# Down projections of 16 experts as three fp32r products, with remainders formed on GpSimd and weight tiles cut by rows

## The chip, the core and the metric

The kernel runs on one core of one Trainium2 chip, as one program. The core has five engines with queues of their own: TensorE (PE), VectorE (DVE), ScalarE (ACT), GpSimd (POOL) and SyncE (SP). Each works through its queue in order; between queues only semaphores order the work. The metric is the device time of one execution in microseconds, as the median of the runs shown. Lower is better.

## The reference

The model is one block of diffusion-style layers (a Fourier branch, a bidirectional mLSTM and, last in the block, a mixture of experts) followed by two attention layers. All of it is float32. The change touches only the mixture of experts. `h` is 1024 rows of 1024 columns, there are 16 experts, and each takes the 128 rows that score it highest:

```python
def expert_choice(h, w_router, w_gate, w_up, w_down):
    b, l, _ = h.shape
    cap = CAP_FACTOR * l // N_EXPERTS                      # 128 rows
    aff = jax.nn.softmax(jnp.einsum('bld,de->ble', h, w_router).astype(jnp.float32), axis=-1)
    vals, idx = lax.top_k(jnp.swapaxes(aff, 1, 2), cap)
    bidx = jnp.arange(b)[:, None, None]
    xs = h[bidx, idx]
    hid = jax.nn.silu(jnp.einsum('becd,edf->becf', xs, w_gate)) * jnp.einsum('becd,edf->becf', xs, w_up)
    y = jnp.einsum('becf,efd->becd', hid, w_down) * vals[..., None].astype(h.dtype)
    return jnp.zeros_like(h).at[bidx, idx].add(y)

x = x + ga2 * expert_choice(hx2, w_router, w_gate_e, w_up_e, w_down_e)
```

Each of `w_gate`, `w_up` and `w_down` is 1024 x 1024 floats (4 MB) for each expert, 12 MB of weights for an expert.

## The kernel before, in words

The order of the work is written out by hand: each engine has its own program, in which an expert is a function `turn(e, more)`, called for expert 1, looped over experts 2 to 14 (`Fori`), and called for expert 15 (`more` is false there, as no expert follows). Expert 0 has gate and up alone ahead of the turns, and `down(16)` ends the stage.

**Tiles.** An expert's weights come in six tiles of 2 MB, numbered j: 0 and 1 gate, 2 and 3 up, 4 and 5 down. Tile j is the column half j % 2 of its matrix with all 1024 rows: 128 partitions x 8 row blocks (k) x 512 columns. `MRAW[j]` is its place; three lie in `ring`, two in `hidden`, one in `pair`. SP loads tile j of the next expert once PE has finished the product with tile j of this one (L758 to L797), in two DMAs of 1 MB. In turn e the down tiles are those of expert e-1.

**Three products.** A gate or up tile is multiplied in fp32r (a float32 rounded for a faster pass of PE) with remainders, whose sum stands for the float32 product. ACT rounds the weights, `high(e, j)`, into `MHIGH[j % 2]`, in four pieces of 128 x 1024 (L1711). DVE subtracts the rounded weights from the raw ones, `low(e, j)` (L2252), in the same four pieces, in place: `MLOW[j]` is the memory of `MRAW[j]`. The gathered rows x are split in the same way into XSH (L1702, ACT) and XSL (L2244, DVE). PE then forms, for each k, xh x high (L1250), xh x low (L1251) and xl x high (L1252), all accumulated in one PSUM bank (`split_product`). There are only two `MHIGH` buffers, so `high(e, j)` for j of 2 or more waits until the product with tile j-2 is done (`moe_high_free`).

**Down.** The down product is float32 (L293, in `group`): hidden rows transposed (`hidT`) times `MRAW[4]` into bank 4, then times `MRAW[5]` into bank 5, 8 matmuls each, and each is two records in the profile.

**PE's turn e:** four products with gate and up tiles of expert e; 8 transposes of the gathered rows of expert e+1 (L1261); down of expert e-1; 8 transposes of the hidden rows of expert e (L1268).

**DVE's turn e:** low of tiles 1, 2, 3; two multiplications of silu(gate) by up (L2259, `hidden_of`); half of the evacuation of the x transposes (L2238) and XSL (L2244); `output(e-1, 0)`, the scaled first half of the down result (L2269, waits for `moe_d`); low of tile 0 of expert e+1; `output(e-1, 1)`; half of the hidden transposes (L2263).

**ACT's turn e:** high of tile 1; silu of gate half 0 (L1719); high 2; silu of half 1; high 3; the other half of the x evacuation (L1693) and XSH (L1702); high 0 of expert e+1; the other half of the hidden transposes (L1715).

**POOL's turn e:** copy the next expert's row numbers (L885) and issue the gather of its rows (L887); wait for both outputs (`moe_y`); copy the row numbers of expert e-1 (L889) and issue the scatter that adds its results to the rows in memory (L891); wait until the scatter has landed (`moe_sct`), which so stands ahead of the next gather.

## Time and profile before

| | us |
|---|---|
| runs of the kernel before | 3163.53, 3164.49, 3170.97 |
| median | 3164.49 |
| the profiled execution, its time | 3172.3 |
| its span, from first to last instruction | 3170.5 |
| expert stage, first gate matmul (L1250) to the last output (L2269) | 1056.9 to 1667.5 |
| busy in the whole span: PE, DVE, ACT, POOL | 2892.3, 1612.7, 1301.3, 120.2 |
| one turn of the loop (L1261 at 1298.69 to L1261 at 1336.12) | 37.43 |

The page's busy shares are means over the whole program. For a change in one stage the views by stretch, by waits and in order of time say more: a row of the timeline gives the start of a group of equal instructions, the time from the first start to the last end, engine, line, what is written and what is read, the count, and in brackets for how long the engine sat idle before it and what ended that. Instructions that overlap are counted from start to start, so four subtractions with a span of 1.22 us each take 4.62 together.

### The profile page before, as it was taken

What the parts mean: (1) busy time and instruction counts of PE and PEld (TensorE: products, weight loads), DVE (VectorE), ACT (ScalarE), POOL (GpSimd) and SP (SyncE); (2) the same over time, 40 slices, a digit from 0 to 9 for tenths busy, and PEclk for the clock granted to TensorE, in tenths of its full rate; (3) what the DMA queues carried; (4) which work ended last, traced back from release to release, by engine and by line L of the source; (5) the groups of instructions that cost most, each with busy time, mean ns of one, the idle gap of its engine ahead of it and who ended that gap; (6) DMA issues with size and microseconds to landing.
All of it is one profiled execution on the core that took longest, in us unless ns stands there. A gap on an engine that the chain in (4) does not pass through costs nothing.

```text
span 3170.5 us, 37695 instructions
## 1 busy us (share of the span) xinstructions
PE 2892.3 (91%) x13850; PEld 2054.6 (65%) x13858; DVE 1612.7 (51%) x3148; ACT 1301.3 (41%) x2426; POOL 120.2 (4%) x168
## 2 busy tenths in 40 slices
PE   7999999999995699999994988898999988999998
PEld 3454467588875566666663765576667775776677
DVE  1217546234366666666644549463643557536433
ACT  2201235223233455445534537553642447436421
POOL 0000000000000010101000000000000000000000
PEclk9999999999996799999997999899999999999999
DMA  9420000122325599999975200200012200200121
GB/s 356 153 80 0 27 27 1 61 99 101 143 104 206 187 352 364 365 367 362 358 247 159 47 14 15 54 27 32 24 54 106 93 2 21 73 17 18 54 80 53
DMA packets 176889, 388.56 MB, mean 123 GB/s; under 512 B 7253, under 2 KB 8309, under 8 KB 176481
## 3 DMA queue, kind: packets, MB, share of 16 engines
q1 hardware_dynamic: 157920, 318.79, 28.7%
q0 software_dynamic: 18672, 67.72, 6.5%
q8 instruction: 97, 1.59, 0.2%
q14 instruction: 56, 0.45, 0.0%
q10 hardware_dynamic: 144, 0.01, 0.0%
HBM read 354.98 MB, written 31.51 MB: 122 GB/s over the span
## 4 chain that ended last, share of the span: by engine, by line
PE 84%; DVE 6%; ACT 4%; DMA 3%; issue 2%; SPq 1%; DVEq 0%; POOL 0%; POOLq 0%; ACTq 0%
PE psum L293 20%; PE psum L707 7%; PE psum L709 7%; PE psum L708 7%; PE psum L1250 4%; PE psum L1252 4%; PE psum L1251 4%; PE psum L1368 4%; PE psum L1386 3%; PE psum L1196 3%; PE psum L1195 3%; PE psum L1194 3%; PE psum L1415 2%; PE psum L1463 2%; PE psum L1465 2%
## 5 line engine op out<-in xcount | busy, mean ns | idle before, releaser
L708 PE MATMUL psum<-ring_r,kctx_r 128*128 128x512 f32 (+1 forms) x544 | 214.0, 393 | 0.0
L708 PE MATMUL psum<-ring_r,cols_r 128*128 128x512 f32 (+1 forms) x544 | 213.6, 393 | 0.0
L1812 ACT ACTIVATE ring<-ring,att 128x256 f32<-128x256 f32 (+7 forms) x256 | 173.7, 679 | 66.1 <-DVE att L2385 66.1
L1368 PE MATMUL psum<-wide 64*128 64x512 f32 (+2 forms) x704 | 155.2, 524 | 22.7 <-DVE att L2385 19.7
L293 PE MATMUL psum<-hidden,ring 128*128 128x512 f32 x384 | 167.5, 597 | 6.0 <-DVE wide L2126 4.0
L2252 DVE TENSOR_TENSOR ring_r<-ring,pair_r 128x1024 fp32r<-128x1024 f32 x128 | 148.1, 1219 | 23.7 <-ACT pair_r L1711 23.7
L1251 PE MATMUL psum<-ring_r,wide_r 128*128 128x512 f32 x384 | 151.3, 394 | 0.0
L1386 PE MATMUL psum<-ident,ring 128*128 128x128 f32 x640 | 120.1, 295 | 26.8 <-ACT sel_wT L1824 16.2
L1386 PEld LDWEIGHTS psum<-ident,ring 128*128 128x128 f32 x640 | 68.8, 143 | 105.4 <-issue 71.4
L293 PEld LDWEIGHTS psum<-hidden,ring 128*128 128x128 f32 x384 | 73.4, 192 | 97.0 <-issue 94.8
L1194 PE MATMUL psum<-small_r,ring_r 128*128 128x512 f32 x320 | 125.8, 393 | 0.8 <-DVE pair L2142 0.8
L1196 PE MATMUL psum<-small_r,ring_r 128*128 128x512 f32 x320 | 126.3, 395 | 0.0
L585 DVE TENSOR_TENSOR ring_r<-ring,ring_r 128x1024 fp32r<-128x1024 f32 x48 | 58.8, 1225 | 129.6 <-ACT ring_r L582 129.2
L1711 ACT ACTIVATE pair_r<-ring 128x1024 fp32r<-128x1024 f32 x128 | 124.5, 1048 | 0.0
L708 PEld LDWEIGHTS psum<-ring_r,kctx_r 128*128 128x128 f32 x544 | 104.9, 193 | 22.4
L708 PEld LDWEIGHTS psum<-ring_r,cols_r 128*128 128x128 f32 x544 | 103.9, 191 | 21.7
L707 PE MATMUL psum<-small_r,kctx_r 128*128 128x512 f32 (+1 forms) x240 | 101.0, 421 | 16.0 <-issue 7.7
L293 PE MATMUL psum<-pair,wide 128*128 128x512 f32 x256 | 112.6, 592 | 1.2 <-DMA pair<-in_w_down 1.2
L293 PE MATMUL psum<-hidden,wide 128*128 128x512 f32 x256 | 112.6, 593 | 1.0 <-DVE wide L2263 1.0
L707 PE MATMUL psum<-small_r,cols_r 128*128 128x512 f32 (+1 forms) x240 | 98.8, 412 | 15.2 <-DVE wide_r L676 13.8
L1250 PE MATMUL psum<-pair_r,wide_r 128*128 128x512 f32 x256 | 102.8, 402 | 7.0 <-DVE wide_r L2244 3.9
L1465 PE MATMUL psum<-wide_r,ring_r 128*128 128x512 f32 x256 | 101.9, 398 | 0.0
(452 smaller groups left out, 6759.8 us busy)
## 6 DMA issues: line engine op xcount, KB each, us to landing
ring<-in_w_gate SPq DMA_DIRECT2D x64, 1024.0 KB, 9.3
ring<-in_w_up SPq DMA_DIRECT2D x32, 1024.0 KB, 9.7
hidden<-in_w_up SPq DMA_DIRECT2D x32, 1024.0 KB, 9.4
hidden<-in_w_down SPq DMA_DIRECT2D x32, 1024.0 KB, 7.3
pair<-in_w_down SPq DMA_DIRECT2D x32, 1024.0 KB, 7.7
ring<-in_w_ada SPq DMA_DIRECT2D x24, 1024.0 KB, 12.1
ring<-in_w_in SPq DMA_DIRECT2D x24, 1024.0 KB, 7.3
ring<-in_even_w_in SPq DMA_DIRECT2D x16, 1024.0 KB, 16.0
```

Source lines behind the costliest of these rows:

```text
L293: mm = pe.matmul(outp, l, r, start=(i == 0), stop=(i == len(pairs) - 1))
L707: self.eng.matmul(outp, XHIGH[b][:, k, :], whigh(key, k)[:, 0:wd], start=(k == 0), stop=False)
L708: self.eng.matmul(outp, XHIGH[b][:, k, :], low[:, k, 0:wd], start=False, stop=False)
L709: mm = self.eng.matmul(outp, XLOW[b][:, k, :], whigh(key, k)[:, 0:wd], start=False, stop=(k == KT - 1))
L1194: pe.matmul(outp, w, high[:, j, :], start=(j == 0), stop=False)
L1196: mm = pe.matmul(outp, lows[:, k, span(c)], high[:, j, :], start=False, stop=(j == kn - 1))
L1250: pe.matmul(outp, xh[:, k, :], high, start=(k == 0), stop=False)
L1251: pe.matmul(outp, xh[:, k, :], low[:, k, :], start=False, stop=False)
L1368: mm = pe.matmul(bank(2 * (q % 2) + h)[:, 0:n], qT2[row, c, span(b)], kT2[row, 0 if name == "C" else c, k:k + n], start=True, stop=not dia ...
L1386: mm = pe.transpose(bank(4)[:, span(k)], sv[:, span(k)], ident[:])
L1465: mm = pe.matmul(bank(j % 4), low[:, k, span(c)], GHIGH[:, k, :], start=False, stop=(k == KT - 1))
L1812: act.activation(sv, sv, ACT.Exp, bias=nmx[:, q:q + 1], scale=-1.0, accum_out=esum[:, r:r + 1]).then_inc(S(name + "_e"), 1)
```

## The change

The changed kernel cuts every matrix by rows: tile j is the row half j % 2, 4 row blocks in full length of 1024 columns, so that a piece of 128 x 1024 is one row block, and both tiles of a matrix add to both of its banks. `split_product` takes, for each piece, both column halves. All that follows gate (silu) or up or down therefore waits for the second tile (`moe_g`, `moe_u`, `moe_d` at 2).

The down product becomes three fp32r products as well: `MSPLIT` is 6, ACT rounds tiles 4 and 5 too, and POOL forms their remainders (L903 of the changed kernel), signalled by `mw_lowd`. The transposed hidden rows are split into HDH (ACT, L1736) and HDL (DVE, L2289). In the last down product, that of turn 16, which no gate and up stand beside, ACT's jobs are numbered 0 and 1.

POOL's wait for the scatter's landing moves from the end of its turn to a place just ahead of the next scatter, so that the next gather is issued without it. The first turn is written out ahead of the loop on ACT and POOL.

```diff
+        def rows_of_tile(v):
+            return v.rearrange("p (k n) -> p k n", n=D)
...
-        MSPLIT = 4
+        MSPLIT = 6
...
+        def moe_lows(eng, e, j, p):
+
+            if j < 4 and not (isinstance(e, int) and e == NEXP):
+                eng.wait_ge(S("mw_low"), e * 16 + (4 * j + p + 1))
+            else:
+                eng.wait_ge(S("mw_lowd"), e * 8 + (4 * (j % 4) + p - 7))
...
-                ms = slice((j % 2) * HALF, (j % 2 + 1) * HALF)
-                w = w[e, :, ms].rearrange("(k p) n -> p k n", p=P) if isinstance(e, int) else \
-                    w[bass.ds(e, 1), :, ms].rearrange("e (k p) n -> p (e k) n", p=P)
-                for k0 in (0, 4):
-                    sp.dma_start(MRAW[j][:, k0:k0 + 4, :], w[:, k0:k0 + 4, :]).then_inc(S(f"ring_full{MRING[j] if j < RING else j}"), 16)
+                rs = slice((j % 2) * HALF, (j % 2 + 1) * HALF)
+                w = w[e, rs, :].rearrange("(k p) n -> p k n", p=P) if isinstance(e, int) else \
+                    w[bass.ds(e, 1), rs, :].rearrange("e (k p) n -> p (e k) n", p=P)
+                for k0 in (0, 2):
+                    sp.dma_start(MRAW[j][:, k0:k0 + 2, :], w[:, k0:k0 + 2, :]).then_inc(S(f"ring_full{MRING[j] if j < RING else j}"), 16)
...
+                for q in range(2):
+                    j = q if isinstance(e, int) and e == NEXP else 4 + q
+                    for p in range(PIECES):
+                        pool.wait_ge(S("mw_high"), moe_pieces(e, j) + (p + 1))
+                        pool.tensor_tensor(MLOW[4 + q][:, p, :], MRAW[4 + q][:, p, :], MHIGH[q][p // 2][:, p % 2, :].bitcast(F32),
+                                           ALU.subtract).then_inc(S("mw_lowd"), 1)
                 pool.wait_ge(S("moe_y"), e * 2)
+                if not isinstance(e, int) or e >= 2:
+                    pool.wait_ge(S("moe_sct"), e * 16 - 16)
                 pool.tensor_copy(idx1[:, 1:2], idxc[:, bass.ds(e - 1, 1)])
                 pool.drain()
                 pool.indirect_dma_start(scratch["acc"], bass.IndirectOffsetOnAxis(idx1[:, 1:2].bitcast(U32), 0), yb, None,
                                         compute_op=ALU.add).then_inc(S("moe_sct"), 16)
-                pool.wait_ge(S("moe_sct"), e * 16)
-
-            with pool.Fori(1, NEXP - 1) as e:
+
+            one(1, True)
+            with pool.Fori(2, NEXP - 1) as e:
                 one(e, True)
             one(NEXP - 1, False)
             one(NEXP, False)
+            pool.wait_ge(S("moe_sct"), NEXP * 16)
...
-            def split_product(e, j, xh, xl, outp):
-
-                low, q = MLOW[j], j % 2
-                for k in range(KT):
-                    if k % PK == 0:
-                        pe.wait_ge(S("mw_low"), moe_pieces(e, j) + (k // PK + 1))
-                    high = MHIGH[q][k // 4][:, k % 4, :]
-                    pe.matmul(outp, xh[:, k, :], high, start=(k == 0), stop=False)
-                    pe.matmul(outp, xh[:, k, :], low[:, k, :], start=False, stop=False)
-                    mm = pe.matmul(outp, xl[:, k, :], high, start=False, stop=(k == KT - 1))
+            def split_product(e, j, xh, xl, slot=None):
+
+                slot = j if slot is None else slot
+                low, q = MLOW[slot], j % 2
+                for p in range(PIECES):
+                    moe_lows(pe, e, j, p)
+                    k = PIECES * q + p
+                    for m in range(2):
+                        outp, ms = bank(2 * (slot // 2) + m), slice(m * HALF, (m + 1) * HALF)
+                        high = MHIGH[q][p // 2][:, p % 2, ms]
+                        pe.matmul(outp, xh[:, k, :], high, start=(k == 0), stop=False)
+                        pe.matmul(outp, xh[:, k, :], low[:, p, ms], start=False, stop=False)
+                        mm = pe.matmul(outp, xl[:, k, :], high, start=False, stop=(k == KT - 1))
                 return mm
...
             def down(e):
 
-                pe.wait_ge(S("moe_hevA"), e)
-                pe.wait_ge(S("moe_hevD"), e)
-                for m in range(2):
-                    moe_full(pe, e, 4 + m)
-                    group(pe, bank(4 + m), [(hidT[:, k, :], MRAW[4 + m][:, k, :]) for k in range(KT)]).then_inc(S("moe_d"), 1)
+                pe.wait_ge(S("moe_hlo"), e * 2)
+                final = isinstance(e, int) and e == NEXP
+                for q in range(2):
+                    split_product(e, q if final else 4 + q, hdh, hdl, slot=4 + q).then_inc(S("moe_d"), 1)
...
             def h_evac(e):
-                act.wait_ge(S("moe_htr"), e * 2 + 1)
-                act.activation(hd[:, 0:HALF], bank(6), ACT.Copy).then_inc(S("moe_hevA"), 1)
+                for m in range(2):
+                    act.wait_ge(S("moe_htr"), e * 2 + (m + 1))
+                    act.activation(HDH[:, m * HALF:(m + 1) * HALF], bank(6 + m), ACT.Copy).then_inc(S("moe_hhi"), 1)
 
             def silu(e, m):
-                act.wait_ge(S("moe_g"), e * 2 + (m + 1))
+                act.wait_ge(S("moe_g"), e * 2 + 2)
...
             def turn(e, more):
                 high(e, 1)
+                high(e, 2)
+                high(e, 3)
                 act.wait_ge(S("moe_hid"), e * 2)
                 silu(e, 0)
-                high(e, 2)
                 silu(e, 1)
-                high(e, 3)
+                high(e, 4)
                 if more:
                     x_evac(e + 1)
                     x_high(e + 1)
+                high(e, 5)
                 if more:
                     high(e + 1, 0)
                 h_evac(e)
 
-            with act.Fori(1, NEXP - 1) as e:
+            turn(1, True)
+            with act.Fori(2, NEXP - 1) as e:
                 turn(e, True)
             turn(NEXP - 1, False)
+            high(NEXP, 0, slot=4)
+            high(NEXP, 1, slot=5)
...
-                dve.wait_ge(S("moe_u"), e * 2 + (m + 1))
+                dve.wait_ge(S("moe_u"), e * 2 + 2)
                 dve.tensor_tensor(hid[:, ms], sgate[:, ms], bank(2 + m), ALU.mult).then_inc(S("moe_hid"), 1)
 
             def h_evac(e):
-                dve.wait_ge(S("moe_htr"), e * 2 + 2)
-                dve.tensor_copy(hd[:, HALF:D], bank(7)).then_inc(S("moe_hevD"), 1)
+                for m in range(2):
+                    ms = slice(m * HALF, (m + 1) * HALF)
+                    dve.wait_ge(S("moe_hhi"), e * 2 + (m + 1))
+                    dve.tensor_tensor(HDL[:, ms], bank(6 + m), HDH[:, ms].bitcast(F32), ALU.subtract).then_inc(S("moe_hlo"), 1)
 
             def output(e, m):
 
                 ms = slice(m * HALF, (m + 1) * HALF)
-                dve.wait_ge(S("moe_d"), e * 2 + (m + 1))
+                dve.wait_ge(S("moe_d"), e * 2 + 2)
```

What stands in a row on POOL in one turn of the loop, before. `kctx` holds the row numbers, `wide` the gathered rows and the results, `moe_y` counts outputs, `moe_sct` landed scatters:

```order
L884 ISA [waits moe_xtr]
L885 ISA [waits moe_gat]
L885 COPY kctx<-kctx 128x1
L887 DMA wide<-scratch_xn,kctx 128x1024
L889 ISA [waits moe_y]
L889 COPY kctx<-kctx 128x1
L891 DMA scratch_acc<-wide,kctx 1024x1024
L895 REGISTER_ALU [waits moe_sct]
```

POOL's turn now, the one written out ahead of the loop (the loop's holds the same, with register instructions between). `hidden_r` and `pair_r` on the left are the remainders of tiles 4 and 5; `pair_r`, `ctx_hidden_r` and `small_r` on the right are ACT's rounded pieces:

```order
L896 COPY kctx<-kctx 128x1 [waits moe_gat,moe_xtr]
L898 DMA wide<-scratch_xn,kctx 128x1024
L903 ISA
L903 TENSOR_TENSOR hidden_r<-hidden,pair_r 128x1024 [waits mw_high] x4
L903 TENSOR_TENSOR pair_r<-pair,ctx_hidden_r 128x1024 [waits mw_high] x2
L903 TENSOR_TENSOR pair_r<-pair,small_r 128x1024 [waits mw_high] x2
L908 COPY kctx<-kctx 128x1 [waits moe_y]
L910 DMA scratch_acc<-wide,kctx 1024x1024
```

Eight subtractions have moved in between the gather and the scatter, each behind a rounding of ACT.

On PE, the x transposes and the down product in a turn of the loop, before:

```order
L1261 MATMUL psum<-ident,wide 128x128 [waits moe_gat]
L1261 MATMUL psum<-ident,wide 128x128 x7
L1293 REGISTER_ALU
L549 ISA [waits moe_hevD,moe_hevA,moe_y]
L293 MATMUL psum<-hidden,wide 128x512 [waits place4]
L293 MATMUL psum<-hidden,wide 128x512 x7
L293 MATMUL psum<-pair,wide 128x512 [waits place5]
L293 MATMUL psum<-pair,wide 128x512 x7
```

The same place now, up to the second piece (there are eight such pieces of six matmuls):

```order
L1284 MATMUL psum<-ident,wide 128x128 [waits moe_gat]
L1284 MATMUL psum<-ident,wide 128x128 x7
L1314 REGISTER_ALU
L564 ISA [waits moe_hlo,moe_y]
L1273 MATMUL psum<-pair_r,wide_r 128x512 [waits mw_lowd]
L1274 MATMUL psum<-hidden_r,wide_r 128x512
L1275 MATMUL psum<-pair_r,cols_r 128x512
L1273 MATMUL psum<-pair_r,wide_r 128x512
L1274 MATMUL psum<-hidden_r,wide_r 128x512
L1275 MATMUL psum<-pair_r,cols_r 128x512
L564 REGISTER_ALU
L1273 MATMUL psum<-pair_r,wide_r 128x512 [waits mw_lowd]
```

Two waits for a loaded tile have become eight waits for a subtraction on POOL.

On ACT, from the second silu to the evacuation of the hidden transposes, now (the turn written out; before, the rows of L1731 that read `hidden` under `place4` and those that read `pair` were not there, and the silus stood between the roundings of tiles 1, 2 and 3):

```order
L1740 ACTIVATE wide<-psum 128x512 [waits moe_g]
L1731 ACTIVATE pair_r<-hidden 128x1024 [waits moe_u,place4]
L1731 ACTIVATE pair_r<-hidden 128x1024 x3
L1714 ACTIVATE wide<-psum,adaT,mod 128x128 [waits moe_xtr]
L1714 ACTIVATE wide<-psum,adaT,mod 128x128 x3
L1723 ACTIVATE wide_r<-wide 128x1024 [waits moe_u,moe_xevD,moe_xevA]
L1731 ACTIVATE ctx_hidden_r<-pair 128x1024 [waits moe_u,place5]
L1731 ACTIVATE ctx_hidden_r<-pair 128x1024
L1731 ACTIVATE small_r<-pair 128x1024 x2
L1731 ACTIVATE pair_r<-ring 128x1024 [waits moe_d,ring_full1]
L1731 ACTIVATE pair_r<-ring 128x1024 x3
L1736 ACTIVATE wide_r<-psum 128x512 [waits moe_htr] x2
```

The rounding of tile 5 stands behind the x evacuation and XSH. DVE's order is as before, apart from L2289, which takes the place of L2263 (two subtractions for one copy); what it waits for has changed.

## Rows read from the trace of the kernel before

**Rows 1.** The page: busy us, share of the span, instructions; granted clock, DMA share.
```profile
PE 2892.3 (91%) x13850; PEld 2054.6 (65%) x13858; DVE 1612.7 (51%) x3148; ACT 1301.3 (41%) x2426; POOL 120.2 (4%) x168
...
PEclk9999999999996799999997999899999999999999
DMA  9420000122325599999975200200012200200121
```

**Rows 2.** Busy time of each engine in two stretches of one turn each.
```profile
core 0: us, PE busy (x) PEld busy (x) DVE busy (x) ACT busy (x) POOL busy (x), PEclk, DMA share, GB/s
...
1281.80:1319.20 37.40, 37.40 (x146) 25.74 (x145) 24.52 (x27) 19.53 (x24) 4.45 (x4) 1.00 1.04 362
1319.20:1356.60 37.40, 37.40 (x145) 25.75 (x144) 24.48 (x27) 19.54 (x24) 3.75 (x4) 1.00 1.04 364
```

**Rows 3.** Waits in the stage, PE's two and SP's two: total, times, longest.
```profile
PE psum L1250 <- DVE ring_r L2252: 3.1, 1, 3.1
PE psum L1268 <- DVE wide L2238: 1.5, 1, 1.5
...
SPq L766 <- PE psum L1252: 232.3, 52, 5.0
SPq L766 <- PE psum L293: 161.3, 26, 6.7
```

**Rows 4.** Timeline of PE, one turn: start, us, line, out<-in, count.
```profile
1298.69 1.04 PE L1261 MATMUL psum<-ident,wide 128*128 128x128 f32 x8
1299.56 7.03 PE L293 MATMUL psum<-hidden,wide 128*128 128x512 f32 x16
1306.43 7.03 PE L293 MATMUL psum<-pair,wide 128*128 128x512 f32 x16
1313.30 1.04 PE L1268 MATMUL psum<-ident,wide 128*128 128x128 f32 x8
...
1314.09 0.48 PE L1250 MATMUL psum<-pair_r,wide_r 128*128 128x512 f32 x1
...
1336.12 1.04 PE L1261 MATMUL psum<-ident,wide 128*128 128x128 f32 x8
```

**Rows 5.** Timeline of ACT behind the x transposes of that turn.
```profile
1299.33 1.51 ACT L1693 ACTIVATE wide<-psum,adaT,mod 128x128 f32<-128x128 f32 x4 [7.02 <-PE psum L1261]
1301.21 1.06 ACT L1702 ACTIVATE wide_r<-wide 128x1024 fp32r<-128x1024 f32 x1 [0.38 <-ACT wide L1693]
1302.18 3.88 ACT L1711 ACTIVATE pair_r<-ring 128x1024 fp32r<-128x1024 f32 x4
```

**Rows 6.** Timeline of DVE from its first output (the first at 1313.50, another turn's).
```profile
1313.50 0.75 DVE L2269 SCALAR_TENSOR_TENSOR wide<-psum,kctx,small 128x512 f32<-128x512 f32 x1 [1.47 <-PE psum L293]
...
1344.17 0.75 DVE L2269 SCALAR_TENSOR_TENSOR wide<-psum,kctx,small 128x512 f32<-128x512 f32 x1 [3.21 <-PE psum L293]
1344.84 4.62 DVE L2252 TENSOR_TENSOR ring_r<-ring,pair_r 128x1024 fp32r<-128x1024 f32 x4
...
1351.80 0.69 DVE L2263 COPY wide<-psum 128x512 f32<-128x512 f32 x1
...
1377.16 1.23 DVE L2244 TENSOR_TENSOR wide_r<-wide,wide_r 128x1024 fp32r<-128x1024 f32 x1 [1.17 <-ACT wide_r L1702]
```

**Rows 7.** POOL: its two copies (ns min/median/max), two with DVE's row beside, its longest.
```profile
L885 POOL COPY kctx<-kctx x14: 183/429/971, 1082.2 to 1587.8; 128x1 int32 x14
...
L889 POOL COPY kctx<-kctx x16: 181/184/185, 1127.6 to 1667.6; 128x1 int32 x14, 128x1 int32<-128x1 int32 x2
...
1136.52 2.35 DVE L2252 TENSOR_TENSOR ring_r<-ring,pair_r 128x1024 fp32r<-128x1024 f32 x2
1137.94 0.97 POOL L885 COPY kctx<-kctx 128x1 int32 x1 [6.87 <-DMA scratch_acc<-wide,kctx]
...
1287.40 1.22 DVE L2252 TENSOR_TENSOR ring_r<-ring,pair_r 128x1024 fp32r<-128x1024 f32 x1
...
1288.05 0.61 POOL L885 COPY kctx<-kctx 128x1 int32 x1 [7.27 <-DMA scratch_acc<-wide,kctx]
...
1315.57 2.65 POOL L891 DMA_INDIRECT scratch_acc<-wide,kctx  x1 [0.87 <-issue]
```

**Rows 8.** The end of the stage: last h transposes on PE, last output on DVE.
```profile
1649.26 1.04 PE L1268 MATMUL psum<-ident,wide 128*128 128x128 f32 x8
...
1666.76 0.75 DVE L2269 SCALAR_TENSOR_TENSOR wide<-psum,kctx,small 128x512 f32<-128x512 f32 x1 [4.91 <-PE psum L293]
```

**Rows 9.** Timeline of PE at the start of the stage, behind an idle stretch.
```profile
1057.54 0.63 PE L1251 MATMUL psum<-ring_r,wide_r 128*128 128x512 f32 x1
1057.96 0.63 PE L1252 MATMUL psum<-pair_r,wide_r 128*128 128x512 f32 x1
```

More of the change, by code:

```diff
@@ L534, in build @@
         SLOT = KT * HALF
-        MRAW = [ringv(q) for q in MRING] + [tile_of(hidden[:, 0:SLOT]), tile_of(hidden[:, SLOT:2 * SLOT]), tile_of(pair[:, 0:SLOT])]
-        MLOW = [tile_of(v) for v in (*(split["ring"][:, q * SLOT:(q + 1) * SLOT] for q in MRING), split["hidden"][:, 0:SLOT],
+        def rows_of_tile(v):
+            return v.rearrange("p (k n) -> p k n", n=D)
+        MRAW = [rows_of_tile(ring[:, q * SLOT:(q + 1) * SLOT]) for q in MRING] + [rows_of_tile(hidden[:, 0:SLOT]), rows_of_tile(hidden[:, SLOT:2 * SLOT]), rows_of_tile(pair[:, 0:SLOT])]
+        MLOW = [rows_of_tile(v) for v in (*(split["ring"][:, q * SLOT:(q + 1) * SLOT] for q in MRING), split["hidden"][:, 0:SLOT],
                                      split["hidden"][:, SLOT:2 * SLOT], split["pair"][:, 0:SLOT])]
-        MHIGH = [[tile_of(split["pair"][:, SLOT:2 * SLOT])[:, 0:4, :], tile_of(split["pair"][:, SLOT:2 * SLOT])[:, 4:8, :]],
-                 [tile_of(split["ctx_hidden"][:, 0:2 * D]), tile_of(split["small"][:, 0:2 * D])]]
+        MHIGH = [[rows_of_tile(split["pair"][:, SLOT:2 * SLOT])[:, 0:2, :], rows_of_tile(split["pair"][:, SLOT:2 * SLOT])[:, 2:4, :]],
+                 [rows_of_tile(split["ctx_hidden"][:, 0:2 * D]), rows_of_tile(split["small"][:, 0:2 * D])]]
         XSH, XSL = split["wide"][:, 7 * D:8 * D], split["wide"][:, 8 * D:9 * D]
-        MSPLIT = 4
+        HDH, HDL = split["wide"][:, 4 * D:5 * D], split["cols"][:, 0:D]
+        MSPLIT = 6
         def moe_full(eng, e, j):
@@ L1241, in _ @@
             pe.wait_ge(S("route"), 1)
[L1243 to L1252 removed]
+            def split_product(e, j, xh, xl, slot=None):
[10 more added lines that the diff above has]
+                        mm = pe.matmul(outp, xl[:, k, :], high, start=False, stop=(k == KT - 1))
                 return mm
[L1255 removed]
+            xsh, xsl, hdh, hdl = (v.rearrange("p (k n) -> p k n", k=KT) for v in (XSH, XSL, HDH, HDL))
             def x_transposes(e):
@@ L1288, in turn @@
                 if more:
-                    pe.wait_ge(S("moe_hevA"), e)
-                    pe.wait_ge(S("moe_hevD"), e)
+                    pe.wait_ge(S("moe_hlo"), e * 2)
                     x_transposes(e + 1)
@@ L1709, in high @@
                 for p in range(PIECES):
-                    ks = slice(PK * p, PK * (p + 1))
-                    act.activation(MHIGH[j % 2][p // 2][:, PK * (p % 2):PK * (p % 2 + 1), :], MRAW[slot][:, ks, :], ACT.Copy).then_inc(S("mw_high"), 1)
+                    act.activation(MHIGH[j % 2][p // 2][:, p % 2, :], MRAW[slot][:, p, :], ACT.Copy).then_inc(S("mw_high"), 1)
             def h_evac(e):
-                act.wait_ge(S("moe_htr"), e * 2 + 1)
-                act.activation(hd[:, 0:HALF], bank(6), ACT.Copy).then_inc(S("moe_hevA"), 1)
+                for m in range(2):
+                    act.wait_ge(S("moe_htr"), e * 2 + (m + 1))
+                    act.activation(HDH[:, m * HALF:(m + 1) * HALF], bank(6 + m), ACT.Copy).then_inc(S("moe_hhi"), 1)
             def silu(e, m):
-                act.wait_ge(S("moe_g"), e * 2 + (m + 1))
+                act.wait_ge(S("moe_g"), e * 2 + 2)
                 act.activation(sgate[:, m * HALF:(m + 1) * HALF], bank(m), ACT.Silu).then_inc(S("moe_sil"), 1)
@@ L1728, in _ @@
             x_high(0)
+            high(0, 2)
+            high(0, 3)
             silu(0, 0)
-            high(0, 2)
             silu(0, 1)
-            high(0, 3)
             x_evac(1)
@@ L2249, in low @@
                 for p in range(PIECES):
-                    ks = slice(PK * p, PK * (p + 1))
                     dve.wait_ge(S("mw_high"), moe_pieces(e, j) + (p + 1))
-                    dve.tensor_tensor(MLOW[slot][:, ks, :], MRAW[slot][:, ks, :],
-                                      MHIGH[j % 2][p // 2][:, PK * (p % 2):PK * (p % 2 + 1), :].bitcast(F32), ALU.subtract).then_inc(S("mw_low"), 1)
+                    dve.tensor_tensor(MLOW[slot][:, p, :], MRAW[slot][:, p, :], MHIGH[j % 2][p // 2][:, p % 2, :].bitcast(F32), ALU.subtract).then_inc(S("mw_low"), 1)
             def hidden_of(e, m):
```

3 lines of the change are left out of this document (1 added, 2 removed).

## The prediction

> **What bounds the kernel now.** The page is read first: TensorE (PE) is busy 91% of the span, and of the four engines it alone is near full [rows 1]. The change touches only the expert stage, from about 1057 to 1667 us, so the next view is that stage in stretches of one turn of its loop. In 37.4 us PE is busy 37.4 us at a granted clock of 1.00, VectorE (DVE) 24.5, ScalarE (ACT) 19.5, GpSimd (POOL) 4 to 4.5, and the DMA engines are never idle [rows 2]. Is PE waiting for those DMAs? The list of waits over the stage has only two rows for PE, 3.1 and 1.5 us; it is SyncE's queue that waits for PE, 232.3 us in 52 waits, before it may refill a tile [rows 3]. So the turn is PE's own work, back to back: from one set of x transposes to the next 1336.12 - 1298.69 = 37.43 us [rows 4]. A change in this stage is worth what it does to this period, times 15 turns (1 to 15), and what it does to the last down product.
>
> **What PE's work becomes.** A down tile of 16 float32 matmul records takes 6.87 us now (1299.56 to 1306.43), two take 13.74. Gate and up are 96 fp32r matmuls from 1314.09 to 1336.12, 22.03 us, 0.2295 us each [rows 4]. The down product as 48 such matmuls is 48 x 0.2295 = 11.0 us: 2.7 us less in a turn. The 96 of gate and up stay 96 (four pieces, two halves, three products in each of four tiles), the transposes stay. If nothing else were late, a turn would take 34.7 us. The tiles' new shape moves the same bytes; as PE doesn't wait for them now [rows 3], I cost it at nothing, and a longer turn only gives them more cover. The gather set free from the scatter's landing is off the path too: PE has no wait for the gather in rows 3.
>
> **What now has to come first.** Every piece of a down tile now needs ACT's rounding (0.97 us, 3.88 for four [rows 5]), then POOL's subtraction, then PE. ACT gains 8 x 0.97 and half an evacuation, about 28 of the turn's us, and stays below PE. POOL gets 8 subtractions of 128x1024 in a turn. Here the trace has no row, so they are bounded by neighbours. Low end: DVE does the same subtraction at 1.14 us in a row (4.62 for four, spans overlap) [rows 6]. High end: POOL's longest instruction in the stage, 2.65 us [rows 7]. My value is 2.3 us, twice the nearest row: the rows of POOL's small copy suggest that POOL reads through something that a DVE instruction with two SBUF inputs occupies. L889, which never meets one, takes 181 to 185 ns; L885 takes 183 to 971, and its long cases end with DVE's subtraction (1137.94 + 0.97 = 1138.91 against 1136.52 + 2.35 = 1138.87; 1288.05 + 0.61 = 1288.66 against 1287.40 + 1.22 = 1288.62) [rows 7]. If both of DVE's reads are open to POOL only one after the other, its subtraction takes 2 x 1.14. I take this sharing to hold both ways.
>
> By the Trainium skill, GPSIMD Engine Reference, section 3, a float32 tensor_tensor of 2048 columns takes 4497 ns on GpSimd; an estimate of half is 2.25 us, and the sum below would be some 6 us less. No run here shows it yet.
>
> **The turn, walked.** Take as zero the end of the down product. DVE's order is unchanged, but L2269 now waits for both down tiles, not the first: it used to finish its first half and low(e+1,0) under the second tile (1344.17 to 1349.5 [rows 6]). Now all of this is behind the down product.
> - 0.2 until DVE sees it (1313.30 to 1313.50), 0.67 first output, 4.6 low(e+1,0), 0.75 second output, 1.3 the two subtractions of h_evac (0.68 each, nearest row L2263's 0.69), then 12 lows for tiles 1 to 3 at 1.15 = 13.8 [rows 6]. Sum 21.3. PE meanwhile starts product 0 at 2.1 (first low piece), not at 0.9 (its h transposes), and product 1 at 8.8 (first piece of low(e+1,1)), not 7.6: two new waits of 1.2 us. Its product 2 ends at 8.8 + 11.0 = 19.8, and the first rounding of down tile 4 is there at 21.0.
> - So POOL starts at about 21.3, behind DVE's last low, and works 8 x 2.3 = 18.4. Between the fourth and the fifth DVE's x_low (1.23 [rows 6]) goes in: +1.2. The roundings of tile 5 are in time: product 3 ends at 25.3, then 3.5 from the first x transpose to ACT's next rounding (1298.69 to 1302.18 [rows 4, 5]) and 0.97 for the piece: 29.8, while POOL's fifth begins at 21.3 + 9.2 + 1.2 = 31.7.
> - PE has the last piece 1.4 us later, 0.2 for two signals.
> Period 21.3 + 18.4 + 1.2 + 1.6 = 42.5 us against 37.43: +5.1, times 15 = +77.
> - The end: from the last h transposes to the last output it is 17.5 us now (1649.26 to 1666.76) [rows 8]. After: 0.2 + 1.4 for turn 15's outputs, 3.7 for its copy, issue and scatter, which stand ahead in POOL's queue (0.18, 0.87 and 2.65 [rows 7]), 18.4 of subtractions, 1.6, and 0.7 to the second output: 26.0. +8.
> Together +85 us: 3172.3 of the profiled execution (span 3170.5, 1.8 around it) becomes 3257. The median of the runs shown, 3164.5, is 7.8 below that execution; so I say 3250.
>
> **Rivals.**
> - *No sharing of reads.* POOL starts at 21.0 and nothing goes in between: 21.0 + 18.4 + 1.6 = 41.0 (the fifth piece is due at 30.2, its rounding is there at 29.8). 3.6 x 15 + 8 = 62: 3234 for the profiled execution, 3227. For it: a single kind of copy shows the sharing. Against: its ends fit to 0.05 us in both rows.
> - The Trainium skill (SBUF — State Buffer, "Who interferes with whom") says that a VectorE instruction with two SBUF inputs and a GpSimd instruction that reads SBUF exclude each other for a whole instruction; by that rule the walk with sharing holds, without it this rival. The copies of this trace agree for POOL's side (0.97 us in place of 0.18); none shows DVE waiting.
> - *POOL still slower, or PE's clock falls in the gaps.* At 2.65 us a piece 16 x 8 x 0.35 = 45 us more, 3295. The clock is 1.00 in the stage now [rows 2], and PE would be idle some 8 of 42 us, in pieces of 1 to 2 us. At 1057 us, after an idle stretch, the same matmuls come every 0.42 us (1057.54 to 1057.96 [rows 9]), the lower of the two levels (1.2 GHz against 2.4); a turn at that pace has 41 us of gate and up alone in place of 22, and the total would pass 3400. Nothing in the rows of the stage speaks for it.
> - *POOL is hidden, no change.* At DVE's 1.14 us a piece POOL is ahead of PE (1.38 per piece), and PE bounds again: 34.7 + 1.2 + 1.2 = 37.1, -0.3 x 15 = -5, last down -3 at most: 3157 to 3162. It decides at about 1.4 us a piece.
> - *Faster.* The same, and low(e+1,0) and h_evac cost PE nothing because DVE gets through them before PE is back from its transposes: 34.7 + 1.2 for one wait left = 35.9, -1.5 x 15 = -23: 3141. It needs POOL under 1.4 us and DVE 1.2 us earlier; DVE's order and rows speak against it.
> - *The change doesn't do what it says* is no open case: the order has the 8 subtractions in POOL's turn and PE's new waits for them.
>
> **How the numbers follow.** Shared reads, 2.1 to 2.5 us a piece: 0.60, 3225 to 3276, likeliest 3250. No sharing: 0.20, 3200 to 3240. Slower still: 0.10, 3290 and up. No change: 0.06. Faster: 0.04. One tenth of a us in POOL's piece is 13 us of the total, which makes the range: 3200 to 3290, leaving out most of the last three cases. A measurement of this kernel can tell about 0.3%, 9.5 us, from no change. Faster by more 0.05, within 0.06, slower by more 0.89.
>
> **What would show it.** In the profile after: POOL's subtraction on L903 with starts 2.2 to 2.4 us apart (1.2: the forecast falls); POOL busy some 290 us more than its 120; PE idle before matmuls of the down products, released by POOL, 6 to 8 us a turn, and by DVE twice a turn, 1.2 us each; x transposes 42 to 43 us apart; DVE's x_low starting only when a POOL subtraction ends (if not, no sharing); down products of 11.0 us only where nothing waits. The forecast is wrong if the period is under 39 us or PE's granted clock in the stage is below 0.95.

## The result and the profile after

| | before | changed |
|---|---|---|
| runs, us | 3163.53, 3164.49, 3170.97, 3164.33 | 3402.95, 3398.98, 3395.34, 3399.03 |
| median | 3164.41 | 3399.01 |
| ratio | | 1.0727, 95% interval 1.071 to 1.0744 |

The kernel is 234.6 us slower, 7.3%. The forecast was slower by 85 us, to 3250, with a range to 3290: the sign was right, the size missing by 149 us. The first view is again the page of the changed kernel, to be read beside [rows 1]:

```profile
span 3400.6 us, 38657 instructions
...
PE 2906.8 (85%) x14106; PEld 2118.3 (62%) x14114; DVE 1617.9 (48%) x3164; ACT 1431.5 (42%) x2570; POOL 599.4 (18%) x296
...
L910 POOL DMA_INDIRECT scratch_acc<-wide,kctx x16 | 213.2, 13325 | 13.9 <-issue 13.9
...
L1284 PE MATMUL psum<-ident,wide 128*128 128x128 f32 x128 | 29.6, 408 | 163.3 <-DMA wide<-scratch_xn,kctx 163.3
L903 POOL TENSOR_TENSOR hidden_r<-hidden,pair_r 128x1024 fp32r<-128x1024 f32 x64 | 150.1, 2432 | 24.3 <-ACT pair_r L1731 23.9
```

POOL is busier by 479 us, not by 290. The subtractions (all of L903) are 308 us of that, close to the forecast; the rest is one line that the change did not touch in itself: the scatter's issue, L910, 13.3 us each on average in place of 2.0. And PE is idle for 163.3 us ahead of the x transposes (L1284), released by the DMA of the gather. In the stretch from 1132 to 1880 us, which holds 14 turns, these rows follow the waits of ACT and DVE for PE (engine, line, what it waited for, total, times, longest):

```profile
...
PE psum L1284 <- DMA wide<-scratch_xn,kctx: 152.1, 13, 13.2
POOL kctx L908 <- DVE wide L2295: 115.9, 15, 8.1
POOL wide L898 <- issue: 115.4, 13, 9.8
...
PE psum L1273 <- POOL pair_r L903: 26.5, 43, 0.7
PE psum L1273 <- DVE ring_r L2277: 25.8, 28, 1.3
```

In [rows 3] PE had no wait for the gather at all. PE's two forecast waits, for POOL and for DVE, are there too, and small, some 2 us a turn each. One turn of the loop, an output of DVE and then POOL's timeline (start, length, instruction, idle time before it):

```profile
1400.28 0.75 DVE L2295 SCALAR_TENSOR_TENSOR wide<-psum,kctx,small 128x512 f32<-128x512 f32 x1 [11.17 <-PE psum L1275]
...
1406.48 0.18 POOL L908 COPY kctx<-kctx 128x1 int32 x1 [8.07 <-DVE wide L2295]
1407.53 14.99 POOL L910 DMA_INDIRECT scratch_acc<-wide,kctx  x1 [0.87 <-issue]
1421.95 0.77 POOL L896 COPY kctx<-kctx 128x1 int32 x1
1431.31 1.00 POOL L898 DMA_INDIRECT wide<-scratch_xn,kctx  x1 [8.59 <-issue]
1432.33 9.29 POOL L903 TENSOR_TENSOR hidden_r<-hidden,pair_r 128x1024 fp32r<-128x1024 f32 x4
1442.34 4.99 POOL L903 TENSOR_TENSOR pair_r<-pair,ctx_hidden_r 128x1024 fp32r<-128x1024 f32 x2 [0.72 <-ACT ctx_hidden_r L1731]
1447.31 4.71 POOL L903 TENSOR_TENSOR pair_r<-pair,small_r 128x1024 fp32r<-128x1024 f32 x2
```

DVE beside it, behind the second output:

```profile
1406.14 1.28 DVE L2289 TENSOR_TENSOR cols_r<-psum,wide_r 128x512 fp32r<-128x512 f32 x2
1407.34 2.35 DVE L2277 TENSOR_TENSOR ring_r<-ring,ctx_hidden_r 128x1024 fp32r<-128x1024 f32 x2
1409.61 2.35 DVE L2277 TENSOR_TENSOR ring_r<-ring,small_r 128x1024 fp32r<-128x1024 f32 x2
1411.88 4.62 DVE L2277 TENSOR_TENSOR ring_r<-ring,pair_r 128x1024 fp32r<-128x1024 f32 x4
1416.42 2.35 DVE L2277 TENSOR_TENSOR hidden_r<-hidden,ctx_hidden_r 128x1024 fp32r<-128x1024 f32 x2
1418.69 2.35 DVE L2277 TENSOR_TENSOR hidden_r<-hidden,small_r 128x1024 fp32r<-128x1024 f32 x2
```

And PE in the same turn:

```profile
1399.97 1.03 PE L1291 MATMUL psum<-ident,wide 128*128 128x128 f32 x8
...
1402.21 0.50 PE L1273 MATMUL psum<-pair_r,wide_r 128*128 128x512 f32 x1 [1.21 <-DVE ring_r L2277]
...
1408.61 0.50 PE L1273 MATMUL psum<-ctx_hidden_r,wide_r 128*128 128x512 f32 x1 [0.64 <-DVE ring_r L2277]
...
1436.80 1.97 PE L1284 MATMUL psum<-ident,wide 128*128 128x128 f32 x8 [11.41 <-DMA wide<-scratch_xn,kctx]
...
1453.56 1.04 PE L1291 MATMUL psum<-ident,wide 128*128 128x128 f32 x8
```

The turn is 1453.56 - 1399.97 = 53.6 us. What the reader is to see is the pair of rows 1407.53 and 1418.69. DVE runs twelve subtractions, two SBUF inputs each, from 1407.34 to 1421.04 with no idle time between. POOL's issue of the scatter starts 0.2 us behind the start of the first of them and ends at 1422.52, 1.5 us behind the last. The kernel before did the same issue in 1.6 to 2.67 us (ns min/median/max):

```profile
L891 POOL DMA_INDIRECT scratch_acc<-wide,kctx x16: 1569/1600/2665, 1128.7 to 1668.7; - x16
```

From there on all is late in one queue: the copy, a drain (it ends only when the scatter has landed, as an experiment below shows), the gather at 1431.31, and only then POOL's own subtractions, which the prediction had starting at 21.3 us after the down product and which start at 1432.33 - 1399.97 = 32.4.

The theory for the experiments, A: POOL's issue needs a moment of an interface through which DVE reads its second SBUF input, and a run of DVE instructions without a pause keeps it out to the end. The rivals: B, the scatter is slow for another reason (loads, its place in the DMA queue); C, the moved wait lets gather and scatter disturb each other; D, it is POOL's own arithmetic.

### The profile page after: what moved, and what is told of

Its sections match the earlier page's. It is cut to its first block, busy times and chain, and to the rows that moved or that the text cites. A ratio compares the mean times of both kernels' runs of the same rounds, so it can differ in the third digit from the quotient of the medians.

```text
span 3400.6 us, 38657 instructions
## 1 busy us (share of the span) xinstructions
PE 2906.8 (85%) x14106; PEld 2118.3 (62%) x14114; DVE 1617.9 (48%) x3164; ACT 1431.5 (42%) x2570; POOL 599.4 (18%) x296
## 4 chain that ended last, share of the span: by engine, by line
PE 63%; POOL 9%; issue 9%; DVE 7%; POOLq 6%; ACT 4%; DMA 2%; SPq 1%; DVEq 0%; ACTq 0%
PE psum L293 12%; PE psum L718 6%; PE psum L720 6%; PE psum L719 6%; POOLq L897 6%; POOL hidden_r L903 4%; POOL pair_r L903 4%; PE psum L1389 3%; PE psum L1407 3%; PE psum L1216 3%; PE psum L1215 3%; PE psum L1214 3%; PE psum L1436 2%; PE psum L1484 2%; PE psum L1486 2%
## 5 line engine op out<-in xcount | busy, mean ns | idle before, releaser
L910 POOL DMA_INDIRECT scratch_acc<-wide,kctx x16 | 213.2, 13325 | 13.9 <-issue 13.9
L1273 PE MATMUL psum<-pair_r,wide_r 128*128 128x512 f32 x384 | 164.1, 427 | 33.3 <-DVE ring_r L2277 20.7
L1284 PE MATMUL psum<-ident,wide 128*128 128x128 f32 x128 | 29.6, 408 | 163.3 <-DMA wide<-scratch_xn,kctx 163.3
L903 POOL TENSOR_TENSOR hidden_r<-hidden,pair_r 128x1024 fp32r<-128x1024 f32 x64 | 150.1, 2432 | 24.3 <-ACT pair_r L1731 23.9
L1731 ACT ACTIVATE pair_r<-ring 128x1024 fp32r<-128x1024 f32 x128 | 124.9, 1048 | 52.9 <-issue 33.1
L1284 PEld LDWEIGHTS psum<-ident,wide 128*128 128x128 f32 x128 | 23.8, 214 | 169.3 <-DMA wide<-scratch_xn,kctx 157.8
```

Source lines behind the costliest of these rows:

```text
L903: pool.tensor_tensor(MLOW[4 + q][:, p, :], MRAW[4 + q][:, p, :], MHIGH[q][p // 2][:, p % 2, :].bitcast(F32), ALU.subtract).then_inc(S("mw_ ...
L910: pool.indirect_dma_start(scratch["acc"], bass.IndirectOffsetOnAxis(idx1[:, 1:2].bitcast(U32), 0), yb, None, compute_op=ALU.add).then_inc( ...
```

## The experiments

Each is a change to the changed kernel, and its diff is cut to the lines that matter. Where a time stands alone it is of one execution; the kernel before took 3167.01 and 3169.68 us beside them, and 3167.79 (median of seven) beside the two timed ones.

**A pause in DVE's run.** DVE waits for its own result behind each subtraction of tiles 1 to 3.

```diff
                     dve.tensor_tensor(MLOW[slot][:, p, :], ..., ALU.subtract).then_inc(S("mw_low"), 1)
+                    if j in (1, 2, 3) and p in (0, 1, 2, 3) and not (isinstance(e, int) and e == 0):
+                        dve.wait_ge(S("mw_low"), e * 16 + (4 * j + p + 1))
```

> Changed kernel, with DVE waiting for the completion of each of its subtractions of tiles 1 to 3 before the next (12 in a turn), so that a short gap lies between two of them; nothing else is changed. Theory A (POOL's issue of the scatter reads SBUF and cannot get in while DVE runs its two-input subtractions without a gap: it takes 14.99 us in the changed kernel, ending 1.5 us after the last of 13.7 us of them): the issue falls to 3 us or less, the scatter lands 10 us after it and not 23, PE no longer waits for the gather (11.4 us a turn), the turn falls from 53.7 to 42.5 to 44 us and the whole to 3240 to 3260 us. Theory B (the scatter is slow for another reason, DMA load or its place in the queue): the issue stays at 15 us and the time at 3399 us or some us above it.

Measured: 3269.91 us, 129 less. POOL's timeline in a turn, and DVE's beside the issue:

```profile
1400.57 0.18 POOL L908 COPY kctx<-kctx 128x1 int32 x1 [8.05 <-DVE wide L2297]
1401.62 2.50 POOL L910 DMA_INDIRECT scratch_acc<-wide,kctx  x1 [0.87 <-issue]
1403.56 1.81 POOL L896 COPY kctx<-kctx 128x1 int32 x1
1413.67 1.89 POOL L898 DMA_INDIRECT wide<-scratch_xn,kctx  x1 [8.30 <-issue]
...
1401.43 2.56 DVE L2277 TENSOR_TENSOR ring_r<-ring,ctx_hidden_r 128x1024 fp32r<-128x1024 f32 x2
1404.12 2.48 DVE L2277 TENSOR_TENSOR ring_r<-ring,small_r 128x1024 fp32r<-128x1024 f32 x2
```

DVE does the same work with 0.12 us of idling between most subtractions, and the issue falls from 14.99 to 2.50 us. B falls. The time is 10 us above the expected range: the turn is 1394.05 - 1349.72 = 44.3 us, not 42.5 to 44. DVE's row is longer, its last two subtractions above all (4.58 us at 1414.81 in place of 2.35, beside POOL's), and PE still waits for the gather, 1.58 us in that turn.

**The same with one pause only**, behind the first subtraction of tile 1.

```diff
+                    if j in (1,) and p in (0,) and not (isinstance(e, int) and e == 0):
+                        dve.wait_ge(S("mw_low"), e * 16 + (4 * j + p + 1))
```

> Changed kernel, with DVE waiting for its own result once in a turn, behind the first subtraction of tile 1, and for nothing else. Theory A (one gap lets one waiting POOL instruction in): the scatter's issue falls from 15 to 3 us, but POOL's copy behind it waits for the end of DVE's run, so the gather is issued some 24 us after the down product's end, and a turn takes about 24 + 18.8 + 1.2 + 1.6 = 45.6 us, 3280 us in all. Rival (POOL needs the interface for most of the scatter's issue, not for a moment): the issue stays near 15 us, 3399 us.

Measured: 3281.18 us. POOL's rows:

```profile
1406.45 2.50 POOL L910 DMA_INDIRECT scratch_acc<-wide,kctx  x1 [0.87 <-issue]
1408.39 1.60 POOL L896 COPY kctx<-kctx 128x1 int32 x1
```

The issue is 2.50 us again: one pause of about 0.1 us in 13.7 us is worth 118 us of the kernel. So it is a moment that the issue needs, not the whole time. The expectation met the time to 1 us, but by luck: POOL's copy did not wait for the end of DVE's run, the gather was issued 19.5 us behind the down product and not 24, and the turn is 44.4 us (h transposes at 1354.49 and 1398.89), not 45.6.

**The gather ahead of the scatter.** On POOL, the gather of expert e+2 is issued behind the subtractions of turn e and ahead of the wait for the outputs.

```diff
                         pool.tensor_tensor(MLOW[4 + q][:, p, :], ...).then_inc(S("mw_lowd"), 1)
...
+                if more:
+                    fetch(e + 2)
                 pool.wait_ge(S("moe_y"), e * 2)
```

`fetch` holds the lines of the gather, which are taken out of their old place; `fetch(2)` stands ahead of turn 1.

> Changed kernel, with the gather of expert e+2 issued on POOL behind the subtractions of turn e and ahead of the scatter, not behind the scatter. Theory A: the scatter's issue still takes 15 us beside DVE's run, but only the subtractions stand behind it: they start 22.6 us after the down product's end, 22.6 + 18.8 + 1.2 + 1.6 = 44.2 us a turn, 3399 - 15 x 9.5 = 3257 us; PE's wait for the gather is gone. Theory C (POOL is slow throughout, whatever the order): the turn stays above 50 us.

Measured in one execution: 3245.95 us, 11 under the expectation. The expectation's theory C, that POOL is slow whatever the order, falls with it. Of several executions:

> The changed kernel with only the gather moved ahead of the scatter, timed: one look gave 3245.95 us. Expected 3235 to 3250 us, which is what the prediction's walk gives for the changed kernel where nothing waits for the gather.

Measured: 3249.03 us median (3245.04 to 3253.11), ratio 1.0247 to the kernel before, interval 1.0227 to 1.0266. PE's waits for the gather are gone, and what remains is nearly the walk of the prediction: in the single execution, of which the rows below are, h transposes at 1380.95 and, by DVE's rows, outputs at 1381.27 and 1424.18, a turn of 42.9 us. The scatter's issue still ends 1.5 us behind DVE's run, but only the subtractions stand behind it. DVE's and POOL's rows show the mirror image:

```profile
1390.02 13.50 POOL L913 DMA_INDIRECT scratch_acc<-wide,kctx  x1 [2.35 <-issue]
...
1367.26 13.25 DVE L2275 TENSOR_TENSOR wide_r<-wide,wide_r 128x1024 fp32r<-128x1024 f32 x1 [1.18 <-ACT wide_r L1728]
...
1369.48 5.27 POOL L904 TENSOR_TENSOR pair_r<-pair,ctx_hidden_r 128x1024 fp32r<-128x1024 f32 x2
1374.17 5.24 POOL L904 TENSOR_TENSOR pair_r<-pair,small_r 128x1024 fp32r<-128x1024 f32 x2
1378.84 1.70 POOL L895 COPY kctx<-kctx 128x1 int32 x1
```

A subtraction of DVE that takes 1.23 us [rows 6] takes 13.25 here: POOL now runs its pieces without a pause until 1379.41, and DVE's, which asked beside the fourth of eight, ends 1.1 us behind the last. Each side holds off the other, and the side with the run of instructions wins.

**Both together.**

> Gaps in DVE's run and the gather issued ahead of the scatter, both. Theory A: what is left is the walk of the prediction, 21.3 + 12 short gaps of 0.1 + 18.8 + 1.2 + 1.6 = 43 to 44 us a turn, 3240 to 3255 us; about the same as with the gaps alone. Theory B: about that of the gather ahead alone, 3257 us, with the issue still at 15 us.

Measured: 3264.81 us, 10 to 25 above the expectation and little better than the pauses alone (3269.91). With pauses the scatter's issue is 2.49 us, but nothing waits for it any more, while DVE's row is longer and POOL's subtractions, too, are interrupted (11.14 us for four, against 9.29). Against the gather's order alone (3245.95 and 3249.03) the remedy that is not needed costs 16 to 19 us.

**The wait for the landing put back.**

```diff
-                if not isinstance(e, int) or e >= 2:
-                    pool.wait_ge(S("moe_sct"), e * 16 - 16)
                 pool.tensor_copy(idx1[:, 1:2], idxc[:, bass.ds(e - 1, 1)])
                 ...
+                pool.wait_ge(S("moe_sct"), e * 16)
```

> Changed kernel, with POOL's wait for the scatter's landing put back behind the scatter, as in the kernel before. If the moved wait does something (theory C: gather and scatter in flight together slow each other), the turn becomes shorter, 45 us or less. Theory A: nothing changes, within 0.3% of 3399 us, since the drain ahead of the gather's issue (23 us in the trace) already ends only when the scatter has landed.

Measured: 3403.66 us, 0.14% from 3399.01. C falls. The third part of the change, the gather freed from the landing, does nothing: the drain that stands ahead of the gather (L897) lasts until the scatter has landed, 23.2 us (median) behind the start of its issue. With the wait put back it is the wait that lasts, and the drain behind it takes 0.33 us. Of the changed kernel (ns min/median/max):

```profile
L897 POOLq DRAIN  x14: 337/22960/23965, 1083.1 to 1785.5; - x14
```

**The down product in float32 again**, on the new row tiles: no roundings and no remainders for down, POOL with gather and scatter alone, DVE's order as in the changed kernel.

```diff
-        MSPLIT = 6
+        MSPLIT = 4
...
-                    split_product(e, q if final else 4 + q, hdh, hdl, slot=4 + q).then_inc(S("moe_d"), 1)
+                    moe_full(pe, e, 4 + q)
+                    for p in range(PIECES):
+                        for m in range(2):
+                            mm = pe.matmul(bank(4 + m), hidT[:, PIECES * q + p, :], MRAW[4 + q][:, p, m * HALF:(m + 1) * HALF], ...)
+                    mm.then_inc(S("moe_d"), 1)
```

> Changed kernel with the down product in float32 as in the kernel before, on the new row tiles: no roundings and no subtractions for down tiles, nothing on POOL but gather and scatter; DVE's order and its waits for both down tiles stay. Theory A: DVE's run without gaps behind the outputs is still there, so scatter and gather are as late as in the changed kernel, and x transposes wait: 36.8 + 0.9 + 13.7 = 51.4 us a turn, about 3380 us, with no arithmetic on POOL at all. Theory D (POOL's own subtractions hold the scatter back): 25.3 + 0.9 + 13.7 = 39.9 us a turn, 3205 us.

Measured: 3390.78 us, 11 above theory A's 3380. POOL's and DVE's rows, and PE's:

```profile
1404.38 14.99 POOL L904 DMA_INDIRECT scratch_acc<-wide,kctx  x1 [0.86 <-issue]
...
1404.19 2.35 DVE L2273 TENSOR_TENSOR ring_r<-ring,ctx_hidden_r 128x1024 fp32r<-128x1024 f32 x2
...
1433.65 1.97 PE L1278 MATMUL psum<-ident,wide 128*128 128x128 f32 x8 [11.40 <-DMA wide<-scratch_xn,kctx]
```

D falls: with no arithmetic on POOL the scatter still takes 14.99 us and PE still waits 11.4 us for the gather. The cause lies in the row tiles and the order that came with them, which this version keeps. As both halves of a result are done only with the second down tile, DVE's outputs and its low 0, which used to be done under the second tile [rows 6], come behind it, by then all of ACT's roundings are ready, and DVE's twelve subtractions close up to a run without a pause.

**A version that is better than both.** DVE takes the remainders of both down tiles, POOL does no arithmetic, the gather stands ahead of the scatter; low 0 of the next expert goes ahead of the outputs, and ACT rounds tile 5 ahead of the x evacuation.

```diff
...
                 low(e, 3)
+                low_down(e, 0)
                 dve.wait_ge(S("moe_htr"), e * 2)
                 hidden_of(e, 0)
                 hidden_of(e, 1)
                 if more:
                     x_evac(e + 1)
+                low_down(e, 1)
+                if more:
                     x_low(e + 1)
+                    low(e + 1, 0)
                 ...
                 output(e - 1, 0)
-                if more:
-                    low(e + 1, 0)
                 output(e - 1, 1)
                 h_evac(e)
```

> An attempt at a version that is better than both: gather ahead of the scatter, no arithmetic on POOL, the remainders of both down tiles on DVE, whose order is low 1, 2, 3, 4, hidden, x evacuation, low 5, x_low, low 0 of the next expert, then both outputs; on ACT tile 5 is rounded ahead of the x evacuation. DVE has 34 us of work in a turn, PE 34.8. If PE bounds: 34.8 to 35.5 us a turn, 3135 to 3145 us. If the weight loads bound (13.6 MB a turn at the 365 GB/s of the kernel before): 37.3 us, 3165 us. If DVE's work doesn't fit: 36 to 38 us.

> The version with all remainders on DVE and the gather ahead of the scatter again, timed: one look gave 3130.94 us with PE busy without a break in a turn of 34.8 us. Expected 3125 to 3135 us, a ratio of 0.987 to 0.990 to the kernel before.

Measured: 3130.94 us in one execution, then 3130.82 us median (3127.48 to 3132.68), ratio 0.9874 to the kernel before, interval 0.9856 to 0.9893. The busy times from 1132 to 1560 us (columns as in [rows 2]), and one turn:

```profile
1132.00:1560.00 428.00, 428.00 (x1967) 352.88 (x1966) 411.73 (x429) 342.48 (x406) 143.97 (x49) 1.00 1.03 391
...
1351.74 1.04 PE L1283 MATMUL psum<-ident,wide 128*128 128x128 f32 x8
1386.54 1.04 PE L1283 MATMUL psum<-ident,wide 128*128 128x128 f32 x8
...
1367.54 10.44 POOL L907 DMA_INDIRECT scratch_acc<-wide,kctx  x1 [0.86 <-issue]
...
1371.88 4.63 DVE L2275 TENSOR_TENSOR ring_r<-ring,pair_r 128x1024 fp32r<-128x1024 f32 x4
1376.86 2.36 DVE L2275 TENSOR_TENSOR hidden_r<-hidden,ctx_hidden_r 128x1024 fp32r<-128x1024 f32 x2 [0.35 <-ACT ctx_hidden_r L1730]
```

PE is busy without a break, and a turn is 34.80 us: the prediction's 34.7 for PE's own work. The DMA engines move 391 GB/s, the same bytes in a shorter turn (364 x 37.43 / 34.80 = 391), so 365 was no bound. DVE is busy 411.73 of 428 us and has little left. The scatter's issue tells the mechanism once more: it ends at 1377.98, 1.5 us behind the start of DVE's first pause, 0.35 us at 1376.51.

**The same with the gather behind the scatter.**

> The same version with the gather behind the scatter again, as in the changed kernel, and nothing else changed. If the order on POOL's queue is what matters: the scatter's issue starts 3.8 us after the down product's end and ends 1.6 us after DVE's first pause, at 14.2, the drain holds the gather's issue to about 23.5 us, it lands at 29, where the x transposes are due at 22.8: 6 us late, about 41 us a turn, 3220 us. If it doesn't matter here: 3131 us.

Measured: 3207.47 us, 77 above the version with the order turned and 13 under the expectation. Rows of POOL and one of PE:

```profile
1370.46 10.45 POOL L904 DMA_INDIRECT scratch_acc<-wide,kctx  x1 [0.87 <-issue]
...
1390.32 1.00 POOL L898 DMA_INDIRECT wide<-scratch_xn,kctx  x1 [8.13 <-issue]
...
1398.07 1.97 PE L1278 MATMUL psum<-ident,wide 128*128 128x128 f32 x8 [8.43 <-DMA wide<-scratch_xn,kctx]
...
1415.58 2.50 POOL L904 DMA_INDIRECT scratch_acc<-wide,kctx  x1 [0.86 <-issue]
```

The loop's turns alternate: one like the first rows, with an issue of 10.45 us and about 45.5 us long, then one with an issue of 2.50 us and 34.8 us long, in which PE does not wait for the gather. The expectation had 41 us in every turn, and the mean of the loop's turns is 40.6. By one execution of this version, the order of two DMA issues in one queue decides here between 1.3% faster and 1.2% slower than the kernel before.

**Remainders of tile 4 on POOL, of tile 5 on DVE.**

> The same with the remainders of down tile 4 on POOL (four pieces at 2.35 us) and those of tile 5 on DVE. DVE has 29.4 us of work. If POOL's four pieces fit beside DVE: as the version with all on DVE or up to 1 us a turn less, 3130 to 3145 us. If DVE's gapless runs and POOL's keep each other out: pieces late by up to 5 us, 38 to 42 us a turn, 3180 to 3240 us.

Measured: 3166.47 us, 36 above all on DVE, and between the two expectations: the engines keep each other out, but for less than feared (37.3 us a turn). DVE's first two subtractions of tile 5 take 6.35 us in place of 2.35, and the scatter's issue, at 14.98 us, stands ahead of POOL's pieces. Relieving DVE by POOL costs more than it relieves.

## Why the prediction was wrong

- **PE's work.** Right. 34.7 us for PE's own turn was measured at 34.80 where nothing else was late.
- **POOL's subtraction at 2.3 us.** Right: 9.29 us for four, 2.32 each; the median length of those of tile 4 is 2358 ns. The Trainium skill's 4497 ns for twice the width (GPSIMD Engine Reference, section 3) gave an estimate of 2.25.
- **The walk over DVE and PE.** Right to 0.2 us as far as it goes. Product 0 at 2.1 after the down product: 2.24 (1402.21). Product 1 at 8.8: 8.64 (1408.61). DVE's last low at 21.3: 21.07. The end of the stage +8: from the last h transposes to the last output 17.5 us before, 25.6 after (1874.3 to 1899.9). Over the 15 turns the first and the last h transposes lie 565.9 us apart (1083.4 to 1649.3) before, 789.4 after (1084.9 to 1874.3), 645.1 with the gather ahead of the scatter (1077.8 to 1722.9): +79, forecast +77. Part of that agreement is luck: the 1.2 us for DVE's x_low between two pieces of POOL was not paid, as x_low got in behind all of them, while POOL's pieces began at 22.0 and not 21.3 and took 18.8 and not 18.4.
- **"The gather set free from the scatter's landing is off the path."** This step failed. It was argued from an absence, "PE has no wait for the gather in rows 3", and so the walk gave POOL's queue ahead of its subtractions (copy, scatter, drain, gather) no time at all: POOL started "behind DVE's last low", at 21.3. Measured: the scatter's issue from 7.56 to 22.5, the drain to 30.6, the gather's issue at 31.3, the subtractions from 32.4 to 52.0, the next turn at 53.6. The gather of the kernel before was not far from being waited for: issued at 1327.23, landed some 7.2 us later at 1334.4, needed at 1336.12 [rows 4], 1.7 us to spare. The change starts the scatter 7.56 us after the down product in place of 2.27 (1315.57 - 1313.30 [rows 7, 4]); even with an issue of 2.50 us PE then waits 1.6 us (pauses throughout) or 3.2 us (one pause) for the gather. And the wait that was to be removed was not what held the gather; a drain in the same place did.
- **The scatter's issue.** Its price is what put the queue on the path: with 2.50 us POOL's subtractions start at 21.5 (1415.59 - 1394.05), as the walk had it, with 14.99 at 32.4. The prediction named 2.65 us for it and only at the end of the stage. It read the sharing from two copies of POOL and charged it in one place, POOL's own subtractions behind DVE's last one. The same rule, put to the other instructions of POOL's queue, would have met the scatter beside twelve subtractions that the prediction itself had written down as 13.8 us in a row. The 2.65 us was of an issue that got in behind one subtraction of DVE.
- **From these two the missing 149 us.** A turn is 53.8 us, with the gather out of the way 42.9; over the 15 turns that is 789.4 - 645.1 = 144 us.
- **The rivals.** "No sharing" (3227) is refuted by a DVE subtraction of 13.25 us beside POOL's run and an issue of 14.99 us that one pause of DVE brings to 2.50. "POOL still slower" names the right engine and the wrong instruction. "The granted clock falls" did not cause it: it is 0.91 and 0.90 in the turns from 1367.7 to 1475.2 us, below the 0.95 that the prediction set as its limit, but it falls behind PE's 11.4 us of idling and is a result of it: with the gather ahead of the scatter, and no such wait, the mean over the whole execution is 0.954 in place of 0.932.

```profile
1367.70:1421.60 53.90, 38.21 (x162) 29.60 (x161) 24.87 (x27) 27.76 (x34) 35.46 (x13) 0.91 0.72 253
1421.60:1475.20 53.60, 38.31 (x162) 29.90 (x161) 24.78 (x27) 27.82 (x34) 35.36 (x13) 0.90 0.70 254
```

- The Trainium skill, SBUF — State Buffer, "Who interferes with whom", has the exclusion of a two-input VectorE instruction and a reading GpSimd one. This case's runs agree, in both directions, and go further: it was a run of twelve that held off one (14.99 us), and what it held off was the issue of an indirect DMA. That the issue reads SBUF, its row numbers for one, is a guess that fits; no run here shows it.

What stays open is when exactly a run of subtractions closes the door. In the kernel before POOL got in behind one subtraction, where DVE's rows show no pause either (1315.57 + 2.65 = 1318.22, 1.5 us behind that subtraction's end at 1316.74). There ACT's rounding for the next subtraction was done 0.2 us before that one started; in the changed kernel it was done 0.9 us or more before, for all twelve. The alternating turns of the version with the gather behind the scatter have both cases in one execution: the issue takes 2.50 us where the next rounding was done 0.35 us ahead and 10.45 where it was 1.1 us ahead. That a subtraction whose wait is met early is what closes the door fits all runs here, and was not tried by itself.

## What to carry to other kernels

Price every instruction of a queue against what its neighbours will do after the change, not only those that the change adds: a DMA issue on GpSimd counts, and a long run of two-input VectorE instructions with no pause, whose inputs are long ready, can hold it off to the run's end. "Nobody waits for it" in a profile is not slack; take the landing time and the time of need, and say how many microseconds lie between. If something must be issued from GpSimd for the critical path, put it ahead of whatever may be held off, and arithmetic on GpSimd beside a busy VectorE last of all.
